# A hybrid attention and MLP layer on eight cores: causal triangles zeroed on GpSimd, a reordered front, three accumulators, top-k spread over tiles

## Time and profile before

| | us |
|---|---|
| three runs | 1196.43, 1199.35, 1201.86 (median 1199.35) |
| profiled execution, its own time | 1195.82 |
| its span (core 0) | 1193.1 |
| spans of the other cores | 1190.1 to 1193.1 |
| busy: TensorE / ScalarE / VectorE / GpSimd | 1136.5 / 625.2 / 619.4 / 67.7 |

### The profile page before, as it was taken

One profiled execution on the slowest core, in us unless ns is written; L12 is line 12 of the kernel. 1 busy time (PEld: TensorE's weight loads), 2 busy tenths in 40 slices (PEclk: granted clock), 3 DMA queues, 4 the chain that ended last, 5 costly groups with the idle time before them and its releaser, 6 DMA issues.

```text
span 1193.0 us, 25370 instructions; the slowest of 8 cores (1190.1 to 1193.1 us)
## 1 busy us (share of the span) xinstructions
PE 1136.5 (95%) x8875; PEld 627.4 (53%) x8991; DVE 619.4 (52%) x1294; ACT 625.2 (52%) x1264; POOL 67.7 (6%) x127
## 2 busy tenths in 40 slices
PE   2998998999999999999999999999999999999997
PEld 2565565676666767754444455444444444444443
DVE  2655666535434332533443466446566564747377
ACT  5646797998999999852222267420211112020354
POOL 0000221221110000000000000000000000000000
PEclk9998998999999999999999999999999999999999
DMA  9962000002020015163042030422211111111034
GB/s 213 241 127 38 7 9 12 4 6 40 11 39 4 2 28 93 44 196 105 1 72 36 23 67 15 80 49 53 37 36 36 36 35 37 36 36 36 1 119 164
DMA packets 18938, 66.31 MB, mean 56 GB/s; under 512 B 4512, under 2 KB 5280, under 8 KB 14592
## 3 DMA queue, kind: packets, MB, share of 16 engines
q0 software_dynamic: 4752, 34.61, 16.5%
q1 hardware_dynamic: 14064, 30.08, 8.0%
HBM read 90.30 MB, written 8.39 MB: 83 GB/s over the span
## 4 chain that ended last, share of the span: by engine, by line
PE 90%; DMA 4%; DVE 2%; issue 2%; ACT 1%; DVEq 0%; SPq 0%; ACTq 0%
PE bank L327 90%; DMA RG<-x 4%; DVE RG L327 2%; ACT RG L327 1%; DVEq L167 0%; DVEq L160 0%; DVE uT L327 0%; SPq L150 0%; DVE arena L327 0%; ACTq L167 0%; SPq L167 0%
## 5 line engine op out<-in xcount | busy, mean ns | idle before, releaser
L327 ACT ACTIVATE RG<-bank 128x512 bf16<-128x512 f32 (+3 forms) x888 | 454.4, 627 | 351.3 <-PE bank L327 347.5
L327 PE MATMUL bank<-uT,arena 128*128 128x512 bf16 x1964 | 470.1, 379 | 3.7 <-DVE arena L327 0.5
L327 PE MATMUL bank<-RG 128*128 128x65 bf16 (+9 forms) x3780 | 331.2, 226 | 13.5 <-DVE RG L327 9.1
L327 PEld LDWEIGHTS bank<-uT,arena 128*128 128x128 bf16 x2048 | 199.6, 98 | 216.3 <-issue 1.8
L327 DVE TENSOR_TENSOR RG<-RG,bank 128x512 f32<-128x512 f32 x320 | 218.8, 687 | 144.5 <-PE bank L327 141.4
L327 PE MATMUL bank<-arena,RG 128*128 128x512 bf16 x1253 | 277.8, 379 | 1.4
L327 PEld LDWEIGHTS bank<-RG 128*128 128x128 bf16 (+3 forms) x3780 | 201.3, 98 | 96.4 <-issue 18.2
L327 PEld LDWEIGHTS bank<-arena,RG 128*128 128x128 bf16 x1280 | 124.6, 98 | 148.3
L327 DVE TENSOR_TENSOR RG<-RG 128x512 bf16<-128x512 f32 (+3 forms) x203 | 120.9, 596 | 155.0 <-ACT RG L327 150.8
L327 ACT ACTIVATE RG<-RG 128x512 f32<-128x512 f32 (+3 forms) x149 | 86.3, 585 | 72.4 <-DVE RG L327 46.7
L327 ACT ACTIVATE RG<-bank,prm_s 128x512 f32<-128x512 f32 x64 | 43.9, 687 | 117.5 <-PE bank L327 112.0
(11 more groups left out here) (37 smaller groups left out, 277.6 us busy)
## 6 DMA issues: line engine op xcount, KB each, us to landing
arena<-wall POOLq DMA_DIRECT2D x32, 1024.0 KB, 10.3
RG<-x SPq DMA_DIRECT2D x32, 512.0 KB, 15.9
out<-RG SPq DMA_DIRECT2D x32, 256.0 KB, 2.2
RG<-c_qx SPq DMA_DIRECT2D x8, 144.0 KB
RG<-wall POOLq DMA_DIRECT2D x1, 1024.0 KB, 12.3
RG<-c_kx SPq DMA_DIRECT2D x4, 144.0 KB
RG<-RG SPq DMA_DIRECT2D x36, 4.0 KB, 1.8
RG<-c_kx SPq DMA_DIRECT2D x8, 64.0 KB, 1.8
```

The source lines that it names most:

```text
L327: return P.emit(eng, lambda e, method=method, kw=kw: getattr(e, method)(**kw), ins, outs, inc)
```

## The change

- **Masks.** `unit_tiles` gets a flag `cut`, set for all `sel` and FoX units. Their mask matmuls go; instead `diag_cut` has POOL set the triangle of each masked 128 x 128 block of `PT` to zero after EXP, with one `affine_select` per tile (one or two blocks). Window units keep their mask matmuls.
- **Pipeline.** `LAG` 4 instead of 2. `o_bank` gives a unit the accumulator that is released first, of three (of two in the last NSA units and in FoX). The credit is cut off at 1.2, and no further filler group begins in a tile in which one has ended.
- **Top-k.** `topk_prep` runs on POOL. Its thirteen VectorE steps per half are put one to a tile, on tiles without a post. The part of the compressed post that adds up importances moves to a later tile of the same `cw`.
- **Output transposes.** `ot_fill(0, 7)` at the last stage becomes `ot_fill(0, 4)` from the first FoX stage on and `ot_fill(4, 3)` in the last.
- **Front.** `identb` is made on POOL by a memset and a select. TM is stored and loaded without its padding (2304 of 4096 columns), KV in four pieces of 1024 columns, one for each `kv_group`. TM, KV and QN are issued at once. A `tm_group` follows its tile one turn later, the key/value and query groups are added after tiles 3, 8 and 12, and the last ones follow the loop.

```diff
-    wall[BLK['KV']] = _std_block(np.concatenate([kc, vc, ks, kw], 1))
-    wall[BLK['TM']] = _std_block(np.concatenate([vs, vw, gate, f_l], 1))
+    wall[BLK['KV']] = np.concatenate([w.reshape(8, 128, 128).transpose(1, 0, 2).reshape(128, 1024) for w in (kc, vc, ks, kw)], 1)
+    wall[BLK['TM'], :, 0:2304] = np.concatenate([vs, vw, gate, f_l], 1).reshape(8, 128, 288).transpose(1, 0, 2).reshape(128, 2304)
...
             if i0 == 0:
                 W.pump(n=1)
                 P.dma('sp', prm[:, :], prm_d)
-                P.dma('sp', identb[:, :], cd['c_ident'])
+                E('pool', 'memset', ap=identb[:, :], constant=1.0)
+                E('pool', 'affine_select', out=identb[:, :], in_=identb[:, :], pattern=[[1, 128]], compare_op=ALU.is_equal, fill=0.0, base=0, channel_multiplier=-1)
+                W.pump(n=3)
...
-        W.pump(n=2, after=[x_tok[1]])
-        W.pump(n=3, after=[x_tok[4]])
...
-            if i % 4 == 3:
-                todo += [(1.0, lambda it=it: tm_group(it)) for it in range(4 * tg, 4 * tg + 4)]
+            if i > 0:
+                todo.append((1.0, lambda i=i: tm_group(i - 1)))
+            if i == 3 or i in (8, 12):
+                tg = (i - 1) // 4
                 todo += [(1.73, lambda j=j, tg=tg: kv_group(tg, j)) for j in range(4)]
...
         COOL = 8
-        LAG = 2
+        LAG = 4
...
+        def diag_cut(pt, at_):
+            n, st = len(at_), at_[-1] - at_[0] or 1
+            blk = pt.rearrange('p (a b) -> p a b', b=128)[:, at_[0]:at_[-1] + 1:st, :]
+            E('pool', 'affine_select', out=blk, in_=blk, pattern=[[0, n], [1, 128]], compare_op=ALU.is_ge, fill=0.0, base=0, channel_multiplier=-1)
...
             for idx, (segs, masks) in enumerate(tl):
+                cuts, masks = (masks, []) if cut else ([], masks)
...
                     E('act', 'activation', out=PT[pt_][:, 0:cols], in_=banks[d['sb']][:, 0:cols], func=AF.Exp)
+                    if cuts:
+                        diag_cut(PT[pt_], [c[0] // 128 for c in cuts])
...
-        def next_o():
-            ctr['O'] += 1
-            return ctr['O'] % 2
+        held = [0, 0, 0]
+
+        def o_bank(first, count, nb=3):
+            b = min(range(nb), key=lambda b: held[b])
+            assert held[b] <= first
+            held[b] = first + count
+            return b
...
-                state['credit'] = min(state['credit'] + want, 2.0)
-                while state['credit'] > 0:
+                state['credit'] = min(state['credit'] + want, 1.2)
+                state['closed'] = False
+                while state['credit'] > 0 and not state['closed']:
...
-            E('dve', 'tensor_tensor', out=score, in0=impacc[:, :, g, :], in1=topkV, op=ALU.mult)
-            E('dve', 'tensor_tensor', out=score, in0=score, in1=topkC, op=ALU.add)
...
+            E('pool', 'tensor_tensor', out=score, in0=impacc[:, :, g, :], in1=topkV, op=ALU.mult)
+            E('pool', 'tensor_tensor', out=score, in0=score, in1=topkC, op=ALU.add)
+
+        def topk_steps(g, half):
+            steps = []
+            for i in range(4 * half, 4 * half + 4):
+                steps.append(lambda i=i: E('dve', 'max', out=mx8, in_=score[:, i, :]))
+                steps.append(lambda i=i: E('dve', 'match_replace', out=sc2, in_to_replace=mx8, in_values=score[:, i, :], imm_value=-1e+30))
+                steps.append(lambda i=i: E('dve', 'max', out=thr[:, i, :], in_=sc2))
...
-            step = (3, 4)[g]
-            for i in range(8):
-                tiles[base + 1 + step * i]['post'].append(lambda g=g, i=i: topk_tile(g, i))
+            at_ = base + 1
             for j, tg in enumerate((2, 3)):
-                F = Fill(base + 1 + step * (4 * j + 3) + LAG + 5, mark['sel', g, tg] - 9)
+                for fn in topk_steps(g, j):
+                    while tiles[at_]['post']:
+                        at_ += 1
+                    tiles[at_]['post'].append(fn)
+                    at_ += 1
+                F = Fill(at_ + LAG + 3, mark['sel', g, tg] - 9)
...
-        ot_fill(0, 7, stage[7] + 4)
+        ot_fill(0, 4, stage[4] + 6)
+        ot_fill(4, 3, stage[7] + 4)
```

More of the change, by code:

```diff
@@ L180 @@
 NBLK = len(_names)
+PIECES = {'TM': [(0, 2304)], 'KV': [(1024 * j, 1024 * j + 1024) for j in range(4)]}
 STREAM = ['TM', 'KV', 'QN', 'W1V', 'FOX0', 'FOX1', 'X2', 'X3', 'FOX2', 'FOX3']
@@ L381, in pump @@
                     pos = self.loaded
-                    if STREAM[pos] in BLK:
-                        P.dma('pool', self.slot_ap(pos), wall_d[BLK[STREAM[pos]]], after=after)
+                    nm = STREAM[pos]
+                    for c0, c1 in PIECES.get(nm, [(0, 4096)] if nm in BLK else []):
+                        P.dma('pool', self.slot_ap(pos)[:, c0:c1], wall_d[BLK[nm], :, c0:c1], after=after)
                     self.loaded += 1
@@ L597, in build_program @@
             fn()
+        tm_group(15)
+        for j in range(4):
+            kv_group(3, j)
         W.release(pos_kv)
@@ L652, in fill_bank @@
         def fill_bank():
-            if now[0] < cmp_end + 4:
+            if now[0] < cmp_end + LAG + 2:
                 return 7
@@ L717, in S, with EXP @@
                         E('pe', 'matmul', inc=end, out=banks[sb_][:, bo:bo + n], lhsT=identb[:, :], rhs=trib[:, mo:mo + n], start=False, stop=end, skip_group_check=True)
-                def EXP(cols=cols, d=d):
+                def EXP(cols=cols, d=d, cuts=cuts):
                     pt_ = ctr['PT'] % NPT
@@ L748, in emit_one @@
                 if f is None:
-                    if not force and t < cmp_end + 4 and t < state['end'] + COOL:
+                    if not force and t < cmp_end + LAG + 2 and t < state['end'] + COOL:
                         return None
@@ L840, in nsa_post, with importance @@
             return f
+        def importance(g, hl, tg, ob):
+            r = epi_rec(ob)
+            idst = impacc[:, 4 * tg - 8:4 * tg - 4, g, :]
+            ti = tmpi[ctr['i'] % 2]
+            ctr['i'] += 1
+            E('dve', 'tensor_tensor', out=idst if hl == 0 else ti, in0=Obv[ob][:, :, 65:97], in1=r.unsqueeze(2).to_broadcast([128, 4, 32]), op=ALU.mult)
+            if hl > 0:
+                E('pool', 'tensor_tensor', out=idst, in0=idst, in1=ti, op=ALU.add)
         def fox_post(h, tg):
@@ L872, in topk_prep @@
         def topk_prep(g):
-            E('dve', 'tensor_tensor', out=score, in0=impacc[:, :, g, :], in1=topkV, op=ALU.mult)
-            E('dve', 'tensor_tensor', out=score, in0=score, in1=topkC, op=ALU.add)
[L876 to L882, removed]
+            E('pool', 'tensor_tensor', out=score, in0=impacc[:, :, g, :], in1=topkV, op=ALU.mult)
[6 more added lines that the diff above has]
+                steps.append(lambda i=i: E('dve', 'max', out=thr[:, i, :], in_=sc2))
+            b = slice(4 * half, 4 * half + 4)
+            steps.append(lambda: E('dve', 'tensor_tensor', out=selbv[:, g, b, :], in0=score[:, b, :], in1=thr[:, b, 7:8].to_broadcast([128, 4, 32]), op=ALU.is_lt))
+            return steps
         def sel_rows(g, tg):
@@ L976, in cw @@
             nv = 65 if tg < 2 else 97
+            at_, wl = len(tiles), window_tiles(tg)
+            wb, cb = o_bank(at_, len(wl) + 1), o_bank(at_ + 1, 3)
             ct = unit_tiles([([(0, 0, 512)], [])], lambda i: kcmpaug[g][tg][0:100, :], QN[g][hl], 100, tg, lambda i: vcmpaug[g][:, 0:nv], nv,
-                            nsa_post(0, h, g, hl, tg), 2)
-            wt = unit_tiles(window_tiles(tg), lambda i: kwaug[g][0:100, i * 128:(i + 1) * 128], QN[g][hl], 100, tg, lambda i: vwaug[:, i, g, :], 65,
-                            nsa_post(2, h, g, hl, tg), next_o())
+                            nsa_post(0, h, g, hl, tg), cb)
+            wt = unit_tiles(wl, lambda i: kwaug[g][0:100, i * 128:(i + 1) * 128], QN[g][hl], 100, tg, lambda i: vwaug[:, i, g, :], 65,
+                            nsa_post(2, h, g, hl, tg), wb)
             tiles += wt[:1] + ct + wt[1:]
+            if tg >= 2:
+                wt[2]['post'].append(lambda: importance(g, hl, tg, cb))
             if tg == 1:
```

35 lines of the change are left out of this document (16 added, 19 removed).

## The result

The changed kernel takes 1188.36 us (median of five runs, 1186.58 to 1189.46) where the kernel before took 1197.82 beside it: a ratio of 0.9922, 95% interval 0.9904 to 0.9939. So it is 9.3 us faster by the ratio.

A forecast was written before the change was run, and what follows sets the result against it. TensorE nearly full, ScalarE idle 38.6 us in the attention (the ceiling), the front bound by arrival, then TensorE. Masks 11.6 + waits 7.2 + clock 3.0 + front 7.0 - new waits 2.0 = 26.8 us, giving 1172.5; range 1158 to 1190.

The forecast's parts named there:

- New waits in the attention: Attention: VectorE waits for `topk_prep` on POOL, and additions before selects in `tg` 1 units, cost 2.0 us, bounds 0 and 6.
- the rival at 1184: Attention and front: ScalarE becomes the bound or the waits move, so only 15 us are gained, 1184 us; chance 0.24.
- the waits move: Attention, part of the rival at 1184: uneven fillers cost, and the waits' removal gives half, 5 us.
- the masks give half: Attention, part of the rival at 1184: removing the mask matmuls gives only 6 us.
- Masks, 11.6: Attention: of 256 mask matmuls taken off TensorE, 212 count at 0.055 us each, 11.6 us gained; bounds 0 and 14.1.
- Select's price: POOL in the attention: a select taken to cost as much as an addition, 0.45 us for one block, 0.67 for two.
- The rival in which POOL is dear: Attention: above 0.75 us a block selects stop TensorE; at 1.6 us the kernel takes about 1239, slower; chance 0.08.
- Accumulators, top-k, credit, 7.2 + 3.0: Attention: these edits remove 7.2 us of waits and burst and 3.0 us of low clock; bounds 4 and 13.
- the clock term: Attention: with the 3.37 us wait gone, at least 6 us at half speed behind it go too, 3.0 us gained.
- Front, 7.0: Front, before the attention: smaller, earlier weight loads start the first `kv_group` at about 21.7, 7.0 us gained; bounds 0 and 10.
- One x tile for each KV piece: Front: four KV pieces of 1.8 us each bring one x tile each, tiles 2 to 5 at about 13, 17, 20, 23.
- The 2.7 us counted for the wait before 61.62: Front: a TensorE wait of 2.16 us and what follows it go, as tile 12 comes earlier; 2.7 us gained.

The follow-up runs named there:

- later: The changed kernel with POOL's addition of an NSA `post` issued three tiles later, behind the selects: 1176.89 us, 0.983 of the kernel before.

## Why the prediction was wrong, step by step

**The step that failed** is the one under "New waits in the attention": "The addition that stands before a select in `tg` 1 units may cost a few tenths, eight times", in the sum as 2.0 us. It costs 11.5 us, shown by moving the addition and nothing else. The mechanism, the units and the number of times (8) were named; the price was not worked out. A hint of it was on record. In `tg` 1 units the first select comes soon after the addition in POOL's queue, and that addition waits for a VectorE `post`; the earlier trace rows showed such a `post` late by 3.37 us behind evictions and top-k steps. POOL's lateness had cost nothing until then, as nobody on TensorE's path waited for POOL. The change made POOL's queue a part of the path, so VectorE's lateness towards POOL came on it as well: 8.2 us of waits, and on seven cores 3.4 us of lost clock behind two of them. The bound of 6 was too low. The range holds the result, but thanks to the rival at 1184, and near its upper end. Of that rival the part "the waits move" is what came; its "the masks give half" is not. The prediction asked only what a select costs, and how much work POOL has in all; its queue order, which it described rightly, carried the price. The other half of this term, `topk_prep` on POOL, made the first `max` of VectorE wait 1.59 and 1.92 us where about 1 us, twice, was counted; what that cost the kernel was not taken apart.

**Masks, 11.6.** Right: 12.4 by the run with all masks back. Start to start (0.055 us each) was the measure to use and not busy time. The difference of 0.8 is within the noise of the two ratios (some 3 us), so it can't tell whether the 44 matmuls that were given nothing gave something.

**Select's price.** 0.29 and 0.41 us, below both additions taken for it; from 128 to 256 columns that is 0.9 ns for each further column. The rival in which POOL is dear is out. The Trainium skill ("GPSIMD Engine Reference", section 3.1) has 1.8 cycles per element for a tight loop and about 12 for data-dependent branching; 0.9 ns is some 1.1 cycles at that page's 1.2 GHz, so the trace is below both and nowhere near the second.

**Accumulators, top-k, credit, 7.2 + 3.0.** Right in size, given that POOL's queue is in order: 3.4 + 4.9 + 1.5 = 9.8 us by the medians, 12.9 by the ratios. In the changed kernel the clock term did not show on seven of eight cores, since the low clock came back behind POOL.

**Front, 7.0.** Wrong: nothing, or a loss of 0.5 to 2.5 (neither clear of the noise). This is the second failing step. Two assumptions broke. "One x tile for each KV piece" gave tiles 2 to 5 at 13, 17, 20 and 23; they are squared at 17.8, 20.6, 24.6 and 29.6. With TM, four KV pieces and QN all issued at once the x tiles come 3 to 7 us later than worked out, tile 6 at 35.2 too, where the earlier trace rows have it at 32.8. And "tile 3 at 17, two ScalarE passes, transposes: 21.7" left out what is queued on ScalarE between the two passes, the squares of a tile not yet landed. With that order turned, 5.2 us came on core 0 (3.4 in the mean of the cores) and 3.47 went to QN ("2.4 us" in the forecast). What the front could give is held by the arrival of QN and tile 6 at about 36 us, where 32 was forecast, and by copies that stand behind tile 6 on ScalarE. The 2.7 us counted for the wait before 61.62 were read from core 0 alone: there the front's end is 1.65 us earlier, 88.35 to 86.7, but before the change the seven other cores ended it at 84.9 to 86.5, and six of them end it 0.6 to 2.0 us later now.

**The signs named.** 80 `trib` matmuls of 128 columns: yes. POOL busy 165: 131.7, selects being cheaper. No wait over 2 us between 110 and 500 and no clock of 0.50: no, as the rows above show. ScalarE idle 15 to 20 us in the attention: 34.2 (22.7 + 3.6 + 7.9 by the stage table), so hardly any of its 38.6 was taken up. The sum had it at 16.8, but had left out its own 2.0 of new waits; with them it is 18.8. First `kv_group` near 22: 30.31. End of the projections near 81: 86.7. End of the attention near 490: 510.3 on core 0, 502.8 at the earliest core. The tail: 676.4, yes. "The forecast is wrong if TensorE or PV waits are put down to POOL": that is what happened. One wait in FoX has no releaser in the profile of the changed kernel, core 0:

```profile
457.05 0.38 PE L327 MATMUL bank<-RG 70*128 70x512 bf16 x1 [2.16 <-issue]
```

A low clock follows it. The third stage gained 2.2 us on that core. On core 1, which has no such stop, it went from 152.2 to 147.0, and on none of the other seven is it longer than 147.8 now. `later` has such a stop on core 6 (2.12 us before 466.77, clock 0.50 behind it) and on core 5. What it is stays open.

**Whether it closes.** 12.4 for the masks and 9.8 (12.9 by the ratios) for the three edits, less 0.5 to 2.5 for the front, is 19.7 to 24.8 us; `later` is 20.7 below the kernel before. Of the 17.5 us by which the forecast gain (26.8) exceeds the measured one (9.3), POOL's order is 9.5 (11.5 where 2.0 stood) and the front 7.5 to 9.5; masks and waits gave about what was forecast, up to 3.5 us more. The times themselves are only 15.9 us apart, because the sum started from 1199.35 and the kernel before took 1197.82 beside the changed one.

## What to carry to other kernels

When work is moved to an idle engine, its idle time is not the question; read what stands ahead of the new instruction in that engine's queue, and how late the input of that has been seen to come, since every such lateness now reaches the path. If it does, move the work that nobody waits for behind the work that somebody does, before touching depth: more lag needs more buffers; here eight were too few for a lag of six, and ten gave 32 us back. And an arrival forecast must follow the tile through each engine's queue in order; where loads are the limit, a reordering moves the wait to the next thing that is late.

## What was not expected of the hardware

A select with an index beside it on GpSimd (294 ns for 128 columns of bf16, 410 for 256) is cheaper than the addition with two inputs in the same trace (673 ns for 256). And a stop of TensorE of about 2 us can cost nearly as much again in clock, or nothing: behind the stops of 1.77 and 2.07 us (before 126.10 and 166.62) the granted clock is 0.50 for a while, 1.7 us lost each time, behind that of 2.40 us (before 205.82) it stays at 1.00. Seven cores of the changed kernel lose 3.4 us in this way; core 6, with the same eight waits, loses none. On core 2 the low clock follows the stops of 2.07 and 2.40 us and not that of 1.77. What decides it is not shown.
